# Feed-forward stage of a decoder step: six rotating product banks, two down-tile banks, and turns in another order

## What is computed

```python
h = _rmsnorm(x, g_pre_ffn) * (1.0 + sc_f) + sh_f
gate, up = jnp.split(jnp.einsum('btd,df->btf', h, w_ffn_in), 2, axis=-1)
f = jnp.einsum('btf,fd->btd', jax.nn.silu(gate) * up, w_ffn_out)
x = x + gt_f * _rmsnorm(f, g_post_ffn)
```

## Time and profile before

| | |
|---|---|
| time, median of 3 runs | 2889.93 us (2884.13 to 2891.91) |
| profiled execution, its own time | 2890.9 us |
| span of the profile | 2888.8 us |
| mean granted TensorE clock | 0.955 |
| PE busy | 2571.6 us, 89% |
| DVE busy | 2006.8 us, 69% |
| ACT busy | 1289.4 us, 45% |
| POOL busy | 1280.2 us, 44% |

### The profile page before, as it was taken

How to read it: one execution, slowest core, us unless ns; L and a number is a source line. 1 busy time by engine, 2 the same in 40 slices (tenths; PEclk the granted TensorE clock), 3 DMA queues, 4 the chain that set the end, 5 groups by cost and what they waited for, 6 DMA issues and landing times. The chain is left out here.

```text
span 2888.8 us, 42580 instructions
## 1 busy us (share of the span) xinstructions
PE 2571.6 (89%) x15492; PEld 2394.7 (83%) x15492; DVE 2006.8 (69%) x2686; ACT 1289.4 (45%) x2228; POOL 1280.2 (44%) x741
## 2 busy tenths in 40 slices
PE   5999999758888959996899999779999977999995
PEld 2999999747777747774799999779999977999995
DVE  2597789657767746744677777787777778777776
ACT  3456545347777754453433333343333334333333
POOL 1575567222323211001666556546655654665561
PEclk8999999979999979997999999889999998999997
DMA  5355445253333236964132222134222213322222
GB/s 213 121 176 168 130 142 173 71 135 84 90 98 94 60 99 196 278 184 122 59 127 73 80 67 88 44 103 147 74 81 67 88 44 102 108 74 80 67 74 85
DMA packets 199097, 315.37 MB, mean 109 GB/s; under 512 B 18210, under 2 KB 156194, under 8 KB 189938
## 3 DMA queue, kind: packets, MB, share of 16 engines
q1 hardware_dynamic: 174578, 295.80, 32.4%
q10 hardware_dynamic: 24320, 16.87, 2.2%
HBM read 266.29 MB, written 46.37 MB: 108 GB/s over the span
## 5 line engine op out<-in xcount | busy, mean ns | idle before, releaser
L2030 POOL TENSOR_TENSOR p_c_lo<-p_graw,p_c_hi 128x512 fp32r<-128x512 f32 x198 | 296.4, 1504 | 265.9 <-ACT p_c_hi L2138 265.9
L2030 POOL TENSOR_TENSOR p_c_lo<-ffn_wraw,p_c_hi 128x512 fp32r<-128x512 f32 x198 | 275.6, 1403 | 293.7 <-ACT p_c_hi L2138 293.7
L328 POOL TENSOR_TENSOR p_w_lo<-p_wraw,p_w_hi 128x1024 fp32r<-128x1024 f32 x100 | 295.6, 2966 | 211.9 <-ACT p_w_hi L389 211.7
L2112 PE MATMUL p_y<-p_f_hi,p_o_hi 128*128 128x342 f32 (+1 forms) x1056 | 341.5, 323 | 14.2 <-POOL p_o_lo L2035 14.2
L2112 PE MATMUL p_y<-p_f_lo,p_o_hi 128*128 128x342 f32 (+1 forms) x1056 | 340.0, 322 | 0.0
L2112 PE MATMUL p_y<-p_f_hi,p_o_lo 128*128 128x342 f32 (+1 forms) x1056 | 339.5, 322 | 0.0
L2355 DVE TENSOR_TENSOR p_y<-p_y 128x342 f32<-128x342 f32 (+1 forms) x480 | 234.3, 507 | 99.5 <-PE p_y L2112 99.5
L349 PE MATMUL p_proj<-p_h_hi,p_w_hi 128*128 128x412 f32 (+1 forms) x800 | 285.1, 356 | 15.5 <-POOL p_w_lo L328 15.2
L349 PE MATMUL p_proj<-p_h_lo,p_w_hi 128*128 128x412 f32 (+1 forms) x800 | 280.2, 350 | 0.0
L349 PE MATMUL p_proj<-p_h_hi,p_w_lo 128*128 128x412 f32 (+1 forms) x800 | 280.2, 350 | 0.0
L2138 ACT ACTIVATE p_c_hi<-p_graw 128x512 fp32r<-128x512 f32 x198 | 119.9, 621 | 341.1 <-DVE p_graw L2292 239.8
(11 more groups left out here) (313 smaller groups left out, 7098.7 us busy)
## 6 DMA issues: line engine op xcount, KB each, us to landing
p_wraw<-w_in SPq DMA_DIRECT2D x100, 512.0 KB, 4.8
p_graw<-w_ffn SPq DMA_DIRECT2D x33, 1024.0 KB, 5.0
ffn_wraw<-w_ffn SPq DMA_DIRECT2D x65, 512.0 KB, 3.6
ffn_wraw<-w_ffn SPq DMA_DIRECT2D x32, 1024.0 KB, 5.3
p_ada<-w_ada SPq DMA_DIRECT2D x32, 512.0 KB, 4.4
z<-p_zout SPq DMA_DIRECT2D x48, 206.0 KB, 2.8
p_ada_ring<-w_ada SPq DMA_DIRECT2D x4, 2048.0 KB, 21.7
p_mix<-mix SPq DMA_DIRECT2D x16, 512.0 KB, 6.1
```

The lines of the kernel that those rows point to most:

```text
L328: pool.tensor_tensor(w_lo[s][:], wraw[:, s, :], w_hi[s][:].bitcast(F32), ALU.subtract).then_inc(lo_done, 1)
L2030: pool.tensor_tensor(c_lo[r][:], source(p), c_hi[r][:].bitcast(F32), ALU.subtract).then_inc(S["lo"], 1)
L2112: mm = pe.matmul(Y[q % YB][:, 0:W], a[s][:, m, :], b[s][:, n, 0:W], start=s == 0 and i == 0, stop=s == 1 and i == 2)
```

## The change

- `YB`, the number of down banks, goes from 4 to 2; the product banks become six, `Z`, and product p = 7u + j goes to bank p % 6. It waits for the `comb` that last reads product p - 6.
- `high_o` and `low_o` of a unit are called at the start of the next unit, for every unit; before they were called in odd units, for u-1 at the start and for u at the end.
- The tree is gone. The sum over the features is taken by eight matmuls with the matrix of ones, one for each slice of the squares in E. The two sums of a group are made after products 0 and 3 of unit t = 1 instead of 3 and 6, and the roots and `gate(·,0)` and `gate(·,1)` are called elsewhere; `gate(·,1)` in unit t = 2.
- One of the two `output` steps of a group goes from DVE to POOL, as one instruction: half 1 in the first two groups, half 0 in the last.
- `low_t(·, 6)` goes from DVE to POOL; the POOL order of `low_t` and `low_w` changes by one place; on DVE the t_adds, low_ts, s1, c11 and the epilogue steps of a turn are called in another order.

The diff, without the tables of semaphore counts (`TD`, `TP`, `EP`):

```diff
@@ -1849,7 +1849,8 @@
 NR = 6
-YB = 4
+YB = 2
+ZB = 6
 NU4 = NGR * FT
@@ -1871,9 +1872,9 @@
             order += pair[sum(counts[:j]):sum(counts[:j]) + c]
-            if u % FT == 1 and u > FT and j in (3, 6):
+            if u % FT == 1 and u > FT and j in (0, 3):
                 spots[u, j].append(len(order))
-                order.append(("sum", group(u) - 1, (3, 6).index(j)))
+                order.append(("sum", group(u) - 1, (0, 3).index(j)))
     for n in range(2):
@@ -1910,9 +1911,8 @@
         f_lo = [buf(f"f_lo{i}", [P, 2, HM], F32R) for i in range(2)]
-        ssum = [buf(f"ssum{n}", [P, HM]) for n in range(2)]
         rstd = [buf(f"rstd{n}", [P, HM]) for n in range(2)]
-        A, B, C, Dk = bank("a"), bank("b"), bank("c"), bank("d")
+        Z = [bank(f"z{i}") for i in range(ZB)]
         Y = [bank(f"y{i}") for i in range(YB)]
@@ -1952,10 +1952,28 @@
         def wait_tp(e, G, name):
-            e.wait_ge(S["t_pool"], len(TP) * G + TP[name])
+            e.wait_ge(S["t_pool"], TP[name, G])
         def wait_ep(e, G, name):
-            e.wait_ge(S["ep"], len(EP) * G + EP[name])
+            e.wait_ge(S["ep"], len(EP) * G + (EP if G + 1 < NGR else EP_LAST)[name])
+
+        def wait_t_low(e, G, j):
+            if j % 2 or not j:
+                wait_td(e, G, f"lo{j}")
+            else:
+                wait_tp(e, G, f"lo{j}")
+
+        def on_pool(G, n):
+            return (n == 1) == (G + 1 < NGR)
+
+        def wait_out(e, G, n):
+            if on_pool(G, n):
+                wait_tp(e, G, "out")
+            else:
+                wait_ep(e, G, "out")
+
+        def summed(e, G, n):
+            e.wait_ge(S["tile"], order.index(("sum", G, n)) + 1)
@@ -1985,18 +2003,18 @@
                 if G:
-                    wait_td(sp, G - 1, "lo6")
-                    wait_tp(sp, G - 1, "lo4")
+                    wait_td(sp, G - 1, "lo5")
+                    wait_tp(sp, G - 1, "lo6")
                 if G >= 2:
...
             def load_x(G, n):
-                wait_ep(sp, G, f"tree{n}")
+                summed(sp, G, n)
                 sp.dma_start(E[n][:, :, 0:HW[G]], io["x1"][:, :, tokens(G, n)]).then_inc(e_in[n], 16)
...
             def store_y(G, n):
-                wait_ep(sp, G, f"out{n}")
+                wait_out(sp, G, n)
                 sp.dma_start(io["yT"][:, :, tokens(G, n)], E[n][:, :, 0:HW[G]]).then_inc(y_out, 16)
@@ -2041,6 +2059,11 @@
                                    ).then_inc(S["t_pool"], 1)
+            def output(G, n):
+                W = HW[G]
+                wait_ep(pool, G, f"scale{n}")
+                pool.wait_ge(e_in[n], 16 * E_LOADS["x", G])
+                pool.tensor_tensor(E[n][:, :, 0:W], E[n][:, :, 0:W], y[:, :, n, 0:W], ALU.add).then_inc(S["t_pool"], 1)
             low_w(0)
@@ -2049,44 +2072,46 @@
             low_w(3)
             low_w(4)
             for u in range(NU4):
-                turn = group(u) + 1 if u % FT == FT - 1 and u + 1 < NU4 else None
-                if u % 2:
+                G, t = group(u), u % FT
+                turn = G + 1 if t == FT - 1 and u + 1 < NU4 else None
+                if u:
                     low_o(u - 1)
                 low_w(NPR * u + 5)
                 low_w(NPR * u + 6)
+                if u == 0:
+                    low_t(0, 6)
+                if G and t == 2:
+                    output(G - 1, 1)
                 low_w(NPR * (u + 1))
+                if G and t == 0:
+                    low_t(G, 6)
                 low_w(NPR * (u + 1) + 1)
+                low_w(NPR * (u + 1) + 2)
                 if turn:
                     low_t(turn, 2)
-                low_w(NPR * (u + 1) + 2)
                 low_w(NPR * (u + 1) + 3)
+                low_w(NPR * (u + 1) + 4)
                 if turn:
                     low_t(turn, 4)
-                low_w(NPR * (u + 1) + 4)
-                if u % 2:
-                    low_o(u)
+            low_o(NU4 - 1)
+            output(NGR - 1, 0)
         @block.tensor
         def _(pe):
             def product(p):
                 u, j = p // NPR, p % NPR
                 G, W, r = group(u), HW[group(u)], p % NR
-                out = (A, Dk, B, C, A, B, C)[j]
+                out = Z[p % ZB]
                 pe.wait_ge(S["lo"], p + 1)
                 if u % FT == 0:
                     pe.wait_ge(S["thi"], NPR * G + j + 1)
-                    if f"lo{j}" in TD:
-                        wait_td(pe, G, f"lo{j}")
+                    wait_t_low(pe, G, j)
+                if p >= ZB:
+                    v, i = (p - ZB) // NPR, (p - ZB) % NPR
+                    if i == 0:
+                        pe.wait_ge(S["p1"], v + 1)
                     else:
-                        wait_tp(pe, G, f"lo{j}")
-                if j < 4:
-                    wait_comb(pe, u - 1, ("t", "u4", "c21", "c12")[j])
-                if j == 4:
-                    pe.wait_ge(S["p1"], u + 1)
-                if j == 5:
-                    wait_comb(pe, u, "c11")
-                if j == 6:
-                    wait_comb(pe, u, "u2")
+                        wait_comb(pe, v, (None, "u4", "c11", "u2", "t", "c21", "c12")[i])
                 i = 0
                 for k in range(4):
                     for a, b in ((c_hi, T_hi), (c_hi, T_lo), (c_lo, T_hi)):
@@ -2114,8 +2139,9 @@
                     W = HW[G]
-                    wait_ep(pe, G, f"tree{n}")
-                    mm = pe.matmul(Y[q % YB][:, 0:W], mods["ones"][:], ssum[n][:, 0:W], start=True, stop=True)
+                    pe.wait_ge(S["sq"], 2 * G + n + 1)
+                    for k in range(KT):
+                        mm = pe.matmul(Y[q % YB][:, 0:W], mods["ones"][:], E[n][:, k, 0:W], start=k == 0, stop=k == KT - 1)
                 mm.then_inc(S["tile"], 1)
@@ -2148,7 +2174,7 @@
                 wait_comb(act, u - 1, "c12")
-                act.activation(pu[:, 0:W], A[:, 0:W], ACT.Copy).then_inc(S["p1"], 1)
+                act.activation(pu[:, 0:W], Z[NPR * u % ZB][:, 0:W], ACT.Copy).then_inc(S["p1"], 1)
@@ -2179,9 +2205,9 @@
                 if G + 1 < NGR:
-                    wait_td(act, G + 1, ("lo5", "lo6")[n])
+                    wait_td(act, G + 1, "lo5")
                     if n == 1:
-                        wait_tp(act, G + 1, "lo4")
+                        wait_tp(act, G + 1, "lo6")
                 else:
@@ -2198,7 +2224,7 @@
                 if G:
-                    wait_ep(act, G - 1, f"out{n}")
+                    wait_ep(act, G - 1, f"scale{n}")
                 act.activation(rstd[n][:, 0:W], Y[q % YB][:, 0:W], ACT.Sqrt, scale=1.0 / D, bias=mods["eps"][:, 0:1]
@@ -2214,17 +2240,15 @@
             for u in range(NU4):
                 G, t = group(u), u % FT
                 turn = G + 1 if t == FT - 1 and u + 1 < NU4 else None
+                ends = G - 1 if G and t == 1 else None
                 if u:
                     silu(u - 1, 1)
-                if u % 2:
                     high_o(u - 1)
                 high_w(NPR * u + 5)
                 if G and t == 0:
                     high_t(G, 6)
-                if G and t == 1:
-                    squares(G - 1, 1)
-                if G and t == 2:
-                    root(G - 1, 1)
+                if ends is not None:
+                    squares(ends, 1)
                 first_product(u)
                 if u:
                     high_f(u - 1, 1)
@@ -2233,13 +2257,17 @@
                     high_t(turn, 0)
                 if u == 0:
                     high_t(0, 4)
+                if ends is not None:
+                    root(ends, 0)
+                if G and t == 2:
+                    gate(G - 1, 1)
                 high_w(NPR * (u + 1))
                 if turn:
                     high_t(turn, 1)
                 if u == 0:
                     high_t(0, 5)
-                if G and t == 1:
-                    gate(G - 1, 0)
+                if ends is not None:
+                    gate(ends, 0)
                 silu(u, 0)
                 high_w(NPR * (u + 1) + 1)
                 if turn:
@@ -2249,22 +2277,19 @@
                 high_w(NPR * (u + 1) + 2)
                 if turn:
                     high_t(turn, 3)
-                if G and t == 1:
-                    root(G - 1, 0)
+                if ends is not None:
+                    root(ends, 1)
                 high_w(NPR * (u + 1) + 3)
                 if turn:
                     high_t(turn, 4)
-                if u % 2:
-                    high_o(u)
                 high_f(u, 0)
                 high_w(NPR * (u + 1) + 4)
-                if G and t == 1:
-                    gate(G - 1, 1)
                 if turn:
                     high_t(turn, 5)
                 if G and t == 0:
                     squares(G - 1, 0)
             silu(NU4 - 1, 1)
+            high_o(NU4 - 1)
             high_f(NU4 - 1, 1)
             for n in range(2):
                 squares(NGR - 1, n)
@@ -2322,8 +2347,9 @@
```

(64 more changed lines are left out.)

10 lines of the change are left out of this document (5 added, 5 removed).

## The result

The changed kernel takes 3009.4 us (median of 4 runs, 3008.6 to 3010.8) where the kernel before takes 2890.9 us (4 runs): ratio 1.041, 95% interval 1.039 to 1.043. It is 118.5 us slower; the forecast was 101 us slower, 2991 us, with a range of 2925 to 3015. The profiled execution took 3008.8 us, its span is 3006.6 us, its mean granted clock 0.955, as before.

The account below looks back on a forecast made before the run. TensorE was taken as full between turns; at turns it waits for VectorE's cg and for o_lo. Steady 67, turns 24, start 3 and end 7 us made +101 on 2890.9, about 2991 us, range 2925 to 3015.

Parts of the forecast that it names:

- steady, 28 pairs: Feed-forward between turns: third tiles wait for late adds with two down banks, 2.4 us a pair, +67 us (59 to 77).
- two turns: Group changes: later o_lo, two small terms and a longer second half cost 12 us each, +24 us (each -5 to +18).
- start: First unit: product (0,6) waits for low_t(0,6), moved to POOL, +3 us (0 to 5).
- end: After the last silu: first of the last tiles waits about 4.3 us for o_hi and o_lo; +7 us (3 to 9).
- ahead: Code outside the feed-forward part: nothing changes there.
- The mechanism: Steady stretch: tile q waits for the add of q-2, so third tiles wait, some 84 times, about 60 us in total.
- Second halves: Turn units t = 1, 2: gate, scale and POOL's output delay the first adds, +8 us a turn.
- first halves: Turn's first half: later high_o delays o_lo for the first down tile, +3.3 us (2 to 4.5), plus 0.7 small terms.
- the forecast's lower bound: Turn's second half: -4 us if POOL's output doesn't block s1.
- Rival B: Steady loss stays (59 to 67 us), but turns win 10 to 15 us each; about 2930 us, chance 0.12.
- Rival C: First add comes 1.6 us earlier, no third tile waits, freed product banks win 54.9 us; 2862 us, chance 0.08.
- Rival D: Each short wait slows the clock for what follows, +50 us over 28 pairs; about 3041 us, chance 0.06.

## Why the prediction came out right

By the steps of the prediction:

| us | forecast | measured |
|---|---|---|
| steady, 28 pairs | 67 (2.4 each) | 86 (3.1 each) |
| two turns | 24 | 27 |
| start | 3 | 2 (4.9 in units 0-2, less one pair's 3.1) |
| end | 7 | 6 |
| ahead | 0 | -3 |
| sum | 101 | 118 |

(2890.9 + 101 is 2992; the prediction has 2991.)

- **The mechanism was right.** Two down banks let the third tile of a run wait for an add that comes late; the experiments with one part undone or done alone show it from both sides, and three banks are enough to end it in the steady stretch. The forecast of three waits a pair, about 84 and 60 us in all, came out at 88 and 53.1 us.
- **The steady term was too small, by 19 us: 3.1 a pair and not 2.4.** In the pair shown, the run after product 2 grew by 2.06 us (forecast 1.75), that after product 4 by 0.42 (0.24), that after product 5 by 0.58 (0.42). The step that was mis-sized is the one from idle time to lost time. I took a wait to cost what lies between the end of the last tile and the first matmul behind it; the matmul behind a wait comes with a restart as well. The idle times shown, 1.35 + 0.16 + 0.30 and 0.39 for `o_lo`, add up to 2.20 us. The four restarts, from the starts of the matmuls, are 0.24 to 0.26 us each, 1.0 together. Of these 0.2 stood in the kernel before already, at the second tile after product 2, again without idle time shown:

```profile
2512.09 0.32 PE L2112 MATMUL p_y<-p_f_hi,p_o_lo 128*128 128x342 f32 x1
2512.37 0.40 PE L2112 MATMUL p_y<-p_f_hi,p_o_hi 128*128 128x342 f32 x1
2512.61 0.32 PE L2112 MATMUL p_y<-p_f_lo,p_o_hi 128*128 128x342 f32 x1
```

2.2 + 1.0 - 0.2 is 3.0 of the 3.1 us. By the experiments, the banks alone cost 2.69 us a pair, where the working has 1.44 + 0.24 + 0.42 = 2.10, and the order 0.42, where it has 0.31; the wait for `o_lo` that the order brings in each pair isn't named in it.
- **The turns: 12.9 and 14.2 where I had 12.** Second halves +7.3 and +7.5 (forecast 8), first halves +5.6 and +6.6 (forecast 4.0). One wait for `o_lo` of 13.43 us stands there where I had named 14, and it ends 3.0 us later than before (forecast 3.3). What the forecast of the first half lacks is a wait in the run after product 3, which it put at nothing. `low_t(·,6)`, now on GpSimd, holds s1 in unit 44, and the first add stands behind it:

```profile
2438.90 3.14 POOL L2060 TENSOR_TENSOR p_T_lo<-p_E,p_T_hi 128x1368 fp32r<-128x1368 f32 x1
```

```profile
2439.39 3.19 DVE L2313 TENSOR_TENSOR p_graw<-p_graw 128x512 f32<-128x512 f32 x1
```

```profile
2443.49 0.43 PE L2137 MATMUL p_y<-p_f_hi,p_o_hi 128*128 128x342 f32 x1 [1.17 <-DVE p_y L2381]
```

This run grew by 1.0 us at the first turn and by 1.5 at this one. In the second half the gate was worth 3.6 us, as costed. GpSimd's `output` took 6.33 us (6.4 forecast) and held s1 for 6.02. That a turn's second half gets shorter if `output` doesn't hold s1, the forecast's lower bound, wasn't seen in the form tried: with the step on VectorE the turn is as long.
- **Start and end** came out within about 1 us, the end with the wait of 4.35 us that was named. At the start product (0,6) does wait for GpSimd's `low_t(0,6)`, 3.75 us; but that instruction had itself waited 4.09 us for ScalarE's `high_t(0,6)`, and moving that one took the loss away.
- **Ahead** had no term. Its 3 us, which came with a higher granted clock there, went the forecast's way by luck.
- **Rival B** (the turns give back 10 to 15 us each) fell: all four turn halves are longer. The turns can give back, but not in this order: with three down banks, and once the gate, the norm and `output` had left the way to the copies, a turn took 125.7 us, 3.6 and 4.8 less than before.
- **Rival C** (faster) asked for the first add 1.6 us earlier, and for the freed product banks to win 54.9 us. Both parts fell: the add is late, and five product banks in the kernel before win nothing. The 54.9 us were no measure of a gain, since a wait taken away at one bank came back at the next.
- **Rival D** (the clock) fell: the granted clock is 1.00, which is the 2.4 GHz level, over the steady stretch with its four short waits a pair.

## What to carry to other kernels

Before a bank is taken from an accumulator's rotation, find for each run of tiles when the first add is done, not only how long it lasts. The rotation needs as many banks as tiles of the run start before that. Here these are three: the run of three after product 2 has its first add done at 2515.33, when its third tile is written already, and the run of four after product 4 has it done at 2523.61, before its fourth tile starts (at about 2524.45, by the rows of the kernel before). One bank too few is paid in every period. Count a wait on a full TensorE as its idle time plus a restart, here about 0.25 us, and look at the starts of the matmuls as well, for a wait can show no idle time at all. And a total of waits for banks doesn't measure a gain: with a fifth product bank the 54.9 us of them fell to 8.2, and the time stayed.
